# Modulation rows of an adaptive norm, split between the token stage's start and its tile loop

## What is computed

```
mod = silu(c) @ ada_w + ada_b            # ada_w: 1024 x 6144
sh1, sc1, ga1, sh2, sc2, ga2 = split(mod, 6)
h = rms_norm(x, norm1_g) * (1 + sc1) + sh1
z = h @ w_in                             # projections, conv, RWKV, spatial gating ...
x = x + ga1 * mix
h = rms_norm(x, norm2_g) * (1 + sc2) + sh2
x = x + ga2 * routed_moe(h)
```

## Time and profile before

| | us |
|---|---|
| median of 3 runs | 4147.47 |
| lowest to highest | 4143.14 to 4159.44 |
| the profiled execution | 4145.14 |
| its span, first to last instruction | 4143.3 |
| TensorE busy in it | 3663.0 (88%) |

### The profile page before, as it was taken

How to read it: one execution, slowest core, us unless ns; L and a number is a source line. 1 busy time by engine, 2 the same in 40 slices (tenths; PEclk the granted TensorE clock), 3 DMA queues, 4 the chain that set the end, 5 groups by cost and what they waited for, 6 DMA issues and landing times. The chain is left out here.

```text
span 4143.3 us, 63261 instructions
## 1 busy us (share of the span) xinstructions
PE 3663.0 (88%) x24883; PEld 2853.4 (69%) x24884; DVE 1207.4 (29%) x2276; ACT 748.9 (18%) x1399; POOL 1186.2 (29%) x1712
## 2 busy tenths in 40 slices
PE   8799999996688989889799999999999927999960
PEld 1566666664688888888689898898988913444430
DVE  0122222222344444444212212122121231222227
ACT  0122222221232223222111111111111101111113
POOL 0133333333555655566210111101111031000013
PEclk9899999998799999999899999999999968999985
DMA  6522222222233223332260111101111134675226
GB/s 244 206 86 86 88 82 81 81 77 107 77 97 96 65 85 97 98 93 69 81 234 34 44 57 39 62 34 44 57 39 62 39 104 164 237 254 189 93 102 213
DMA packets 273319, 424.40 MB, mean 102 GB/s; under 512 B 123100, under 2 KB 174020, under 8 KB 273094
## 3 DMA queue, kind: packets, MB, share of 16 engines
q1 hardware_dynamic: 250616, 348.23, 25.0%
q0 software_dynamic: 13040, 43.54, 3.2%
q10 hardware_dynamic: 9444, 29.30, 1.8%
HBM read 287.98 MB, written 133.02 MB: 102 GB/s over the span
## 5 line engine op out<-in xcount | busy, mean ns | idle before, releaser
L1692 PE MATMUL c_ps<-c_hT,c_wg 128*128 128x128 f32 x6528 | 752.8, 276 | 25.1 <-DMA c_wg<-in_w_in 25.1
L1692 PEld LDWEIGHTS c_ps<-c_hT,c_wg 128*128 128x128 f32 x6528 | 744.0, 193 | 33.0 <-issue 29.5
L640 PE MATMUL a_ps<-a_win,a_hT 128*128 128x512 f32 (+1 forms) x1088 | 416.2, 540 | 3.6 <-DVE a_mix L560 3.4
L2121 PE MATMUL e_ps<-expert_up,e_xT 128*128 x784 | 347.4, 596 | 2.3 <-DVE e_xT L2083 2.3
L634 PE MATMUL a_ps<-a_hT,a_win 128*128 128x128 f32 x2992 | 344.1, 277 | 1.6 <-ACT a_hT L384 1.6
L634 PEld LDWEIGHTS a_ps<-a_hT,a_win 128*128 128x128 f32 x2992 | 340.9, 193 | 5.6 <-issue 2.7
L640 PEld LDWEIGHTS a_ps<-a_win,a_hT 128*128 128x128 f32 x1088 | 204.0, 190 | 199.8 <-issue 187.0
L1036 POOL TENSOR_TENSOR b_tmp<-b_tt,b_ta 128x126 f32<-128x126 f32 (+22 forms) x527 | 202.2, 384 | 325.8 <-DMA b_ta<-s_a 269.2
L2121 PEld LDWEIGHTS e_ps<-expert_up,e_xT 128*128 128x128 f32 x784 | 149.3, 191 | 191.8 <-issue 191.8
L1692 PE MATMUL c_ps<-c_wo,c_mT 128*128 128x512 f32 x544 | 236.3, 592 | 0.0
L1039 POOL TENSOR_TENSOR b_tt<-b_tt,b_tmp 128x126 f32<-128x126 f32 (+22 forms) x527 | 213.3, 405 | 41.3
(11 more groups left out here) (301 smaller groups left out, 5246.2 us busy)
## 6 DMA issues: line engine op xcount, KB each, us to landing
expert_up<-in_exp_w SPq DMA_DIRECT2D x32, 1024.0 KB, 9.9
s_D<-a_oD SPq DMA_DIRECT2D x34, 768.0 KB, 6.0
b_f<-s_D SPq DMA_DIRECT2D x34, 768.0 KB, 7.6
s_yr<-e_yo ACTq DMA_DIRECT2D x49, 512.0 KB, 3.1
m_w<-in_ada_w SPq DMA_DIRECT2D x12, 2048.0 KB, 7.9
b_f<-s_A SPq DMA_DIRECT2D x34, 512.0 KB, 5.8
expert_down<-in_exp_w SPq DMA_DIRECT2D x16, 1024.0 KB, 12.2
s_A<-a_oA SPq DMA_DIRECT2D x17, 768.0 KB, 3.4
```

What stands on the lines that cost most here:

```text
L640: ins = nc.tensor.matmul(ps[:, bank, 0:width], hT[b][:, k, :], win[:, k, c:c + width], start=k == 0, stop=k == KD - 1)
L1692: return nc.tensor.matmul(out, lhsT, rhs, start=start, stop=stop)
L2121: return nc.tensor.matmul(out, lhsT, rhs, start=start, stop=stop)
```

## The change

`stage_modulation` is gone. The token stage does its work in two parts.

In its start, SP loads the vectors, the 30 rows of bias, gain and convolution weights, x of tile 0, and only the first four chunks of `ada_w` (rows sh1 and sc1), in between and behind them the projection weights; the 18 parameter loads move from ScalarE's queue to SP's, between F2's and F3's weights. TensorE uses the chunks as weights, 128 columns at a time, with the two vectors as moving columns, so that the result has the features on partitions at once.

The other 4096 columns are cut into 32 pieces of 128. In each of tiles 0 to 15 VectorE sums two pieces: a piece is loaded (1024 x 128, 512 bytes a run) into the one buffer `aw`, and for each of the 8 slices and both vectors one operation multiplies by the vector's entry and accumulates. TensorE then sums over the partitions with a column of ones (`late_sums`, after F3), VectorE copies the sums into `modT`, and in the last tile one transpose turns them into rows, to which bias and gain are added; they go to DRAM as `late`, and the merge and combine stages broadcast from there. Some buffers of the token stage share one tensor with the chunks' two buffers.

```diff
+        shared = sb("a_shared", [P, 16 * W])
+        cw = [shared[:, 8 * W * i:8 * W * (i + 1)].rearrange("p (k n) -> p k n", k=KD) for i in range(2)]
...
 SP, start:
                 load_x(0, 0)
+                load_ada(0)
+                load_ada(1)
+                load_group("F1")
+                for n in (2, 3):
+                    sp.wait_ge(s["ada_ps"], n - 1)
+                    load_ada(n)
+                load_group("K")
                 load_x(1, 1)
...
+                for name in ("SV", "F2"):
+                    load_group(name)
                 for dst, src in loads:
-                    act.dma_start(dst, src).then_inc(s["prm_in"], 16)
+                    sp.dma_start(dst, src).then_inc(s["prm_in"], 16)
+                for name in ("F3", "R", "V"):
+                    load_group(name)
+                load_late(0)
 SP, a tile:
                     if left >= 2:
                         after(sp, s["xn_ok"], t)
                         load_x(t + 2, b)
+                    if left > 0:
+                        sp.wait_ge(s["part_ok"], t * 4 + 2)
+                        load_late(t * 2 + 1)
...
                     after(sp, s["hT_ok"], t, 2)
                     sp.dma_start(tile_of(scr["h"], t), ...
                     after(sp, s["conv_ok"], t)
                     after(sp, s["sgu_ok"], t)
                     sp.dma_start(tile_of(scr["cs"], t), ...
+                    if left > 1:
+                        sp.wait_ge(s["part_ok"], t * 4 + 4)
+                        load_late(t * 2 + 2)
 VectorE:
+                def late_part(c, i, at):
+                    dve.wait_ge(s["aw_in"], at * 16 + 16)
+                    if i == 0:
+                        freed(dve, s["late_ps"], c)
+                    for k in range(KD):
+                        for v in range(2):
+                            own = part[:, 2 * i + v, :]
+                            if k == 0:
+                                ins = nc.vector.tensor_scalar(own, aw[:, 0, :], sil[:, 8 * v:8 * v + 1], None, ALU.mult)
+                            else:
+                                dve.wait_ge(s["acc_ok"], at * 14 + 2 * (k - 1) + v + 1)
+                                ins = nc.vector.scalar_tensor_tensor(own, aw[:, k, :], sil[:, 8 * v + k:8 * v + k + 1], own,
+                                                                     ALU.mult, ALU.add)
+                            ins.then_inc(s["acc_ok"] if k < KD - 1 else s["part_ok"], 1)
...
                     if not last:
                         mean_square(t + 1)
+                        for i in range(2):
+                            late_part(t, i, t * 2 + i)
...
                     after(dve, s["cc_ok"], t)
 TensorE:
+                for n in range(4):
+                    pe.wait_ge(ada_in[n % 2], 16 * (n // 2 + 1))
+                    for j in range(4):
+                        a = 2 * (4 * n + j)
+                        for k in range(KD):
+                            ins = nc.tensor.matmul(ps[:, B7, a:a + 2], cw[n % 2][:, k, j * P:(j + 1) * P], both[:, k, :],
+                                                   start=k == 0, stop=k == KD - 1)
+                    ins.then_inc(s["ada_ps"], 1)
+
+                def late_sums(t):
+                    pe.wait_ge(s["part_ok"], t * 4 + 4)
+                    after(pe, s["lo_ok"], t)
+                    for i in range(4):
+                        ins = nc.tensor.matmul(ps[:, B_F1, 384 + i:385 + i], part[:, i, :], ones[:, 0:1], start=True, stop=True)
+                    ins.then_inc(s["late_ps"], 1)
...
                     by_feature(B_F3, (CB, CB + P, CSU, CSU + P), b).then_inc(s["F3"], 1)
+                    if not last:
+                        late_sums(t)
...
                     by_token(B7, CR, W, b).then_inc(s["R"], 1)
```

More of the change, by code:

```diff
@@ L122, in clear @@
         self.nc.all_engine_barrier()
[L125 to L224, removed]
@@ L260, in stage_tokens @@
         CBSU = sb("a_cbsu", [P, 4, P])
[L261 to L264, removed]
+        shared = sb("a_shared", [P, 16 * W])
+        cw = [shared[:, 8 * W * i:8 * W * (i + 1)].rearrange("p (k n) -> p k n", k=KD) for i in range(2)]
+        Ks, kk0, ksq, m1 = (shared[:, W * i:W * (i + 1)] for i in range(4))
         SV = sb("a_sv", [P, 256])
@@ L277, in stage_tokens @@
         lxb = sb("a_lxb", [P, W])
-        oA = sb("a_oA", [P, 3, W])
-        oD = [sb(f"a_oD{d}", [P, 3, W]) for d in range(2)]
-        oO = sb("a_oO", [P, 2, W])
+        oA = shared[:, 4 * W:7 * W].rearrange("p (k n) -> p k n", k=3)
+        oD = [shared[:, (7 + 3 * d) * W:(10 + 3 * d) * W].rearrange("p (k n) -> p k n", k=3) for d in range(2)]
+        oO = shared[:, 13 * W:15 * W].rearrange("p (k n) -> p k n", k=2)
         tw = [oD[d][:, 2, :] for d in range(2)]
         ta = ag
-        oC = sb("a_oC", [P, 4, P])
+        oC = shared[:, 15 * W:16 * W].rearrange("p (k n) -> p k n", k=4)
+        crow, prow = CBSU[0:16, 1, :], CBSU[0:30, 0, :]
+        sig, sil = sb("a_sig", [P, 16]), sb("a_sil", [P, 16])
+        aw = sb("a_aw", [P, KD, P])
+        part = sb("a_part", [P, 4, P])
+        ones = sb("a_ones", [P, 2])
+        modT = sb("a_modT", [P, 2, 32])
+        late_b, late_m, late, ind = (aw[0:64, i, :] for i in range(4))
         B_T, B_F1, B_F2, B_F3, B5, B6, B7 = 0, 2, 3, 4, 5, 6, 7
@@ L374, in sum_squares, with _ @@
+                over_tiles(sp, step)
+                sp.wait_ge(s["late_ok"], 1)
+                sp.dma_start(scr["late"], late).then_inc(s["stL"], 16)
+                sp.wait_ge(s["stL"], 16)
+                for name in ("stC", "stA", "stD0", "stD1", "stO"):
+                    sp.wait_ge(s[name], 16 * NT)
+                sp.wait_ge(st_h[0], 16 * 9)
+                sp.wait_ge(st_h[1], 16 * 8)
+            @block.scalar
+            def _(act):
                 def sum_squares(t, b, n):
@@ L387, in evacuate_h @@
                     ins.then_inc(s["hT_ok"], 1)
+                act.wait_ge(s["cT"], 1)
+                nc.scalar.activation(sig[:, :], ps[:, B5, 0:16], ACT.Sigmoid).then_inc(s["sig_ok"], 1)
                 sum_squares(0, 0, 0)
@@ L532, in step @@
                         .then_inc(s["kk_ok"], 1)
+                    if isinstance(t, int) and t == 0:
+                        dve.wait_ge(s["prm_in"], 16 * 18)
                     for d, bw, ba in ((0, B6, B7), (1, B5, B6)):
@@ L669, in step @@
                     by_feature(B_F3, (CB, CB + P, CSU, CSU + P), b).then_inc(s["F3"], 1)
+                    if not last:
+                        late_sums(t)
+                    else:
+                        after(pe, s["lo_ok"], t)
+                        nc.tensor.transpose(ps[0:64, B_F1, 384:512], modT[:, :, :].rearrange("p v c -> p (v c)"), ident)\
+                            .then_inc(s["turn_ps"], 1)
                     freed(pe, s["g_ok"], t)
```

154 lines of the change are left out of this document (108 added, 46 removed).

## The result

The changed kernel takes 4244.3 us (median of 4 runs, 4236.3 to 4251.4), the kernel before beside it 4151.7 (4 runs): a ratio of 1.022, 95% interval 1.019 to 1.025. It is slower, as forecast, but by more than twice as much: the two profiled executions have spans of 4143.3 and 4234.5 us, 91.2 apart, where 35 were forecast.

The account below looks back on a forecast made before the run. TensorE, busy for 88% of the span, was taken to bound the kernel. 66 us won at the start, 100 lost in fifteen tiles and 1 at the last tile made +35, giving 4182 us, range 4112 to 4240.

Parts of the forecast that it names:

- The piece: VectorE's work on one late piece, 16 operations, two pieces a tile: 4.1 us each.
- S: Time of SP's cs store in a tile, from which the chain of late loads and pieces is counted.
- The end: Last tile's added transpose, five small loads and one 32 KB store: 1 us, bounds 0 to 2.1.
- The rival in which a short stall keeps its clock: Tiles 1 to 15: 2.6 + 1.1 us a tile, 56 us lost, net -9, 4138 us; chance 0.22.
- -66 + 100 + 1: Whole kernel, in us: 66 won at the start, 100 lost in fifteen tiles, 1 lost at the last tile.
- I take full clock: Start, early chunks on TensorE: 0.118 us a product, 7.6 us a chunk at full clock.
- the fourth rival: Start: TensorE stays at 1.2 GHz through the early chunks; 53 us won, net +48, 4195 us; chance 0.10.
- The queue is not what holds the second load.: Each tile's second late load: lands 4.6 us after issue; TensorE waits 2.6 us, bounds 0.6 to 4.2.
- 1.3, bounds 0 and 2.5: Second late piece in each tile: at least one of POOL's two products comes in between, 1.3 us a tile.
- 1.1 with their issue (1.9 cold): TensorE's four sums with one moving column, after F3: 1.1 us a tile, 1.9 at the low clock.
- The clock, 1.7: TensorE's clock falls after the stall in each of fifteen tiles: 1.7 us a tile, 0 to 3.4.
- The signs I named: Marks of being right: F1 of tile 0 near 51, V near 113, a tile period of 57 to 58 us.

Follow-up runs that it names:

- e1: Changed kernel with a second buffer for the second late piece, both loads issued behind the cs store; 4102.0 us, ratio 0.987 to the kernel before.
- e2: Changed kernel with only the sums, and the copy that reads them, moved from behind F3 to behind V; 4100.1 us, ratio 0.987 to the kernel before.
- e6: Changed kernel with POOL's first product with k held back until the tile's second piece is done; 4204.1 us, ratio 1.012 to the kernel before.
- e3: Changed kernel with SP issuing the next tile's first late load ahead of the stores of h and cs; 4173.9 us, ratio 1.004 to the kernel before.
- e4: Changed kernel with the early products back in the earlier form, two vectors as weight and 512 moving columns; 4214.7 us, ratio 1.016 to the kernel before.

## Why the prediction was right and wrong

**Right: the sign and the mechanism.** The tiles lose more than the start gains, through one buffer whose filling hangs on the cs store and on the first piece, a wait ahead of the sums, POOL beside the second piece, and a clock that falls behind each wait. e1 and e2 take the wait away from two sides, and nothing of the loss stays but the sums. The piece was priced at 4.1 us and took 4.2 (456.92 to 461.1), F3 was put at S + 15.7 and ended at S + 15.8, the first piece's start at about S + 5 and came at S + 5.5 (S + 4.9 to 5.5 in the fifteen tiles). The end was put at 1 us and is 1.1.

By the Trainium skill, "TensorE: Matmul & The Clock Gate", section "HAM oscillation — how this bites in real kernels", the throttle of a wait in a loop is paid in every round. The trace agrees: granted 0.93 from 130 to 1020 us, and R with V at 15.5 to 16.3 in each of the fifteen tiles where 13.90 was the rule. The rival in which a short stall keeps its clock is out for these waits, none of which is under 3.47 us. Shorter ones went either way: in e3, behind waits of 1.7 to 2.0 us, R with V took 13.98 in four tiles and 15.4 to 17.0 in the others.

**Wrong: the size, in five terms.** The forecast had -66 + 100 + 1; the profile has -53 + 141 + 1, and 2 in the stages behind.

1. *"I take full clock"*, for the early chunks. I carried over 0.118 us a product; they took 54.74 / 256 = 0.214. It is the fourth rival, which had 0.10. That its bound (V near 126, 53 us won) is what came is luck in part: the bound had F3 end near 111 and no wait behind it, where F3 ended at 101.3 and a wait of 7.56, the sums and a slow R and V made up the difference. With the clock back (e4) V of tile 0 stands at 114.1 and its pieces are done at 95.5, where the sum had 113.1 and 96.4. I reasoned from the idle lead in front of the work, where the form of the work differed: in e4, after the same lead, the chunks with 512 moving columns run at 7.03 each from the third on.
2. *"The queue is not what holds the second load."* The first load came as priced, so that its piece began at S + 5.2 on average. The second landed later: its piece began 5.5 to 6.6 us after the issue (8.1 in one tile), where 4.6 was priced like the first. I had moved x by no more than its new place; it took 7.8 us instead of 6.9, the stores ahead of it were still under way too, and the second load behind them took 6.1 (5.6 in the tile with the short wait: issued 402.68, piece from 408.29). This makes the wait without POOL 3.9 (e6), not 2.6.
3. *POOL, "1.3, bounds 0 and 2.5"*: it measures 1.5 on average (5.4 - 3.9), but no tile has that. Either both products get in and the piece is about 2.0 longer (ten tiles), or neither does and it is not longer at all (five).
4. *The sums, "1.1 with their issue (1.9 cold)"*: they stand behind the wait and so run at the low clock, 1.7. I had both numbers and chose the wrong one for a group that, by my own forecast, follows an idle engine. Without the wait it is 0.8 (e1), and in the last of the fifteen tiles, where the clock fell only behind the sums, 0.9.
5. *The clock, 1.7*: 2.1 measured.

A tile: 3.9 + 1.5 + 1.7 + 2.1 + 0.2 (how the wait is counted) = 9.4, where 6.7 was forecast. Every one of the terms went up; the second load is the largest of them. The signs I named show it: F1 of tile 0 at 69 and not 51, V at 126 and not 113 (though under 130), a period of 58.4 or 61.3 instead of 57 to 58. The range's top of 4240 was 4 us short.

## What to carry to other kernels

Idle time of an engine is a place for work only if the result can be late: look up where it is asked for, and first try to ask later (e2, a few lines: from 2.2% slower to 1.3% faster). Where one buffer is filled twice for one consumer, write down the chain load, use, load, use from the event that starts it, with the transfers that stand ahead on that queue, before counting the engine's time. A wait in the middle of TensorE's stream can be paid twice, once itself and once in the clock and in whatever runs directly behind it: here every wait of 3.5 us and more was, while the 0.2 us that it waits for VectorE in each tile left the clock at 1.00 (e1).

## What the runs showed that I had not expected

**Uninterrupted work at half speed.** The window over the early products of the changed kernel:

```profile
12.00:66.00 54.00, 54.00 (x255) 54.00 (x255) 0.00 (x0) 0.00 (x0) 0.00 (x0) 1.00 0.77 276
```

TensorE is busy 54.00 of 54 us. Yet a product of two moving columns takes 0.214 us, where the sums of one moving column take 0.95 / 8 = 0.12 at full clock and 1.86 / 8 = 0.23 at 0.50, and F2 with F3, which load a weight for each product too, 14.45 / 128 = 0.11 with 128 columns. The 1.00 of this window is no record (the first is at 73.3 us). F1 of tile 0, begun at 69.00, fits 1.2 GHz up to that point: 48 products in 7.65 us, where they take 5.62 at full clock (e1, e2 and e3 in the middle tiles); half of the 4.3 us before 73.3 would be 2.1 lost. In e4 the chunks with 512 columns come down to 7.03 us each after some 15 us. It is no accident of one run: the profiles of all five kernels with the two-column form (the changed one, e1, e2, e3, e6) have 54.74 or 54.75 us for the 256 products. What it is in the form that keeps the clock low was not tried further.

**VectorE and POOL: all or nothing.** In the tile at 468.44 POOL was released 1.04 us after the second piece had begun, got both products (L590, L592) in, and VectorE lost 2.0 us. In the tile at 409.94 it was released 1.65 us after (the piece from 408.29), and its product lasted 3.63 instead of 1.26: it ended 1.1 us after the piece (408.69 + 3.76 = 412.45), about its own length. VectorE lost nothing. It is the same in every tile of the changed kernel and, from tile 1 on, of e4, read from the two engines' timelines: where POOL was released 1.62 us or less after the piece's start (or before it) it got in, where 1.65 or more it stood until the piece's end. e2 fits it as well (in up to 1.60, out from 1.72). That is why the tiles come in two lengths, 61 and 58 us. Whether it is also why one kernel's executions differ was not looked at. What lies behind that border was not tried.

The Trainium skill, "SBUF — State Buffer", section "SBUF: two separate sides", says that VectorE and POOL share one pair of ports, and that whichever instruction starts first holds it to its end. The 1355 ns of a VectorE operation beside POOL's 1.26 us agree with that. That POOL stood through some nine operations of VectorE (2.5 us at 3.76 / 14 each) goes beyond it: the rule is about single instructions, and which engine began its run of them first does not tell the two tiles apart, since that was VectorE in both.
